# Modulation columns moved in the weight plan, and four stages of a two-block kernel reordered

## The reference

```python
# first block
mix = jax.nn.sigmoid(gate_na) * y_na + jax.nn.sigmoid(gate_hg) * y_hg   # y_na = attention @ w_na_out
h = h + mix @ w_o[l]                                                    # y_hg = recurrence @ w_hg_out
m = rms_norm(h, norm_mlp[l])
h = h + jnp.square(jax.nn.relu(m @ w_up[l])) @ w_down[l]
# modulation, once in each layer of the second block; c is one vector of 1024
ada = jax.nn.silu(c) @ ada_w + ada_b
shift, scale, gate = jnp.split(ada, 3, axis=-1)
h = rmsnorm(x, norm_g) * (1.0 + scale[:, None, :]) + shift[:, None, :]
# even layer: a window sum over 2, 4, 8 or 16 tokens less the token itself, by groups of 256 columns
outs.append(win_sum / count[None, :, None] - af[..., sl])
z = jnp.einsum('hts,bnshd->bnthd', w, vh) + b_s.T[None, None, :, :, None]   # w is masked, lower triangle
# odd layer
yc = rmsnorm(yc, gla_norm_g).reshape(B_, S, GLA_VW)      # yc: gated linear attention
y = jnp.concatenate([yc, yd], axis=-1) * jax.nn.silu(gate)
```

## Time and profile before

| what | us |
|---|---|
| median of 3 runs | 856.7 |
| the three runs | 856.07, 856.7, 861.47 |
| the profiled execution | 856.8 |
| its span, from the first instruction to the last | 854.8 |
| TensorE busy in the span | 830.4 |
| VectorE busy | 629.7 |
| ScalarE busy | 490.9 |
| GpSimd busy | 109.5 |

### The profile page before, as it was taken

One profiled execution on the slowest core, in us unless ns is written; L12 is line 12 of the kernel. 1 busy time (PEld: TensorE's weight loads), 2 busy tenths in 40 slices (PEclk: granted clock), 3 DMA queues, 4 the chain that ended last, 5 costly groups with the idle time before them and its releaser, 6 DMA issues.

```text
span 854.8 us, 16987 instructions
## 1 busy us (share of the span) xinstructions
PE 830.4 (97%) x6904; PEld 807.8 (95%) x6904; DVE 629.7 (74%) x1002; ACT 490.9 (57%) x876; POOL 109.5 (13%) x130
## 2 busy tenths in 40 slices
PE   5999999999999999999999999999999999999996
PEld 5998899997998999999999999999999999999996
DVE  5676578982899788787999687786888558455663
ACT  6454456664556656564666663544677356666652
POOL 0010255320112000000030420000202030000001
PEclk9999999999999999999999999999999999999999
DMA  9833334453468898989777456565655436544431
GB/s 352 319 100 117 120 124 128 146 179 97 145 225 289 289 389 270 382 281 384 268 250 280 148 184 207 172 198 177 195 160 185 124 102 212 164 156 155 148 103 50
DMA packets 46876, 170.40 MB, mean 199 GB/s; under 512 B 5200, under 2 KB 5456, under 8 KB 46544
## 3 DMA queue, kind: packets, MB, share of 16 engines
q1 hardware_dynamic: 46080, 165.31, 58.3%
q10 hardware_dynamic: 720, 4.01, 1.2%
HBM read 168.26 MB, written 1.05 MB: 198 GB/s over the span
## 4 chain that ended last, share of the span: by engine, by line
PE 82%; DVE 10%; ACT 4%; issue 2%; DMA 1%; POOL 0%; SPq 0%; DVEq 0%; POOLq 0%; ACTq 0%
PE bank L194 81%; DVE wl L233 5%; DVE raw L221 1%; ACT wh L203 1%; DMA raw<-in_ws 1%; DVE B1l L221 1%; ACT L209 1%; PE bank L197 0%; ACT sq L200 0%; DVE A L221 0%; DVE B0l L233 0%; ACT B1h L200 0%; DVE B1l L233 0%; ACT th L200 0%; DVE h L221 0%
## 5 line engine op out<-in xcount | busy, mean ns | idle before, releaser
L233 DVE TENSOR_TENSOR wl<-raw,wh 128x1024 fp32r<-128x1024 f32 x259 | 327.5, 1276 | 21.8 <-ACT wh L203 21.0
L203 ACT CAST wh<-raw 128x1024 fp32r<-128x1024 f32 x259 | 268.9, 1048 | 120.7 <-PE bank L194 60.4
L194 PE MATMUL bank<-XAh,wl 128*128 128x256 f32 (+1 forms) x896 | 255.8, 285 | 2.7 <-DVE wl L233 2.1
L194 PE MATMUL bank<-XAl,wh 128*128 128x256 f32 (+1 forms) x896 | 249.9, 279 | 0.0
L194 PE MATMUL bank<-XAh,wh 128*128 128x256 f32 (+1 forms) x896 | 249.8, 279 | 0.0
L194 PEld LDWEIGHTS bank<-XAh,wl 128*128 128x128 f32 x896 | 168.7, 188 | 6.0 <-DVE wl L233 2.7
L194 PEld LDWEIGHTS bank<-XAl,wh 128*128 128x128 f32 x896 | 169.3, 189 | 0.0
L194 PEld LDWEIGHTS bank<-XAh,wh 128*128 128x128 f32 x896 | 168.7, 188 | 0.1
L194 PE MATMUL bank<-B1h,wl 128*128 128x256 f32 (+1 forms) x464 | 130.7, 282 | 3.3 <-DVE wl L233 2.1
L194 PE MATMUL bank<-B1h,wh 128*128 128x256 f32 (+1 forms) x464 | 129.8, 280 | 0.0
L194 PE MATMUL bank<-B1l,wh 128*128 128x256 f32 (+1 forms) x464 | 129.7, 280 | 0.0
(11 more groups left out here) (261 smaller groups left out, 1228.0 us busy)
## 6 DMA issues: line engine op xcount, KB each, us to landing
raw<-in_ws SPq DMA_DIRECT2D x307, 512.0 KB, 4.4
bias<-in_bias ACTq DMA_DIRECT2D x1, 1664.0 KB, 12.0
hK<-in_xk SPq DMA_DIRECT2D x4, 272.0 KB, 4.8
h<-in_xt ACTq DMA_DIRECT2D x1, 1088.0 KB, 6.4
out<-gc SPq DMA_DIRECT2D x4, 256.0 KB, 2.6
C<-in_cst SPq DMA_DIRECT2D x1, 512.0 KB, 7.6
crow<-in_crow ACTq DMA_DIRECT2D x1, 512.0 KB, 3.5
wT<-in_wt SPq DMA_DIRECT2D x1, 512.0 KB, 6.5
```

Of the source, the lines that this page charges most:

```text
L194: return self.real.matmul(*a, **k)
L203: return self.real.copy(*a, **k)
L233: return self.real.tensor_tensor(*a, **k)
```

## The change

Five edits, none of which alters what is computed or how many products there are.

1. The line in `plan` that places the 48 items "a". Before, they stand after units 58 to 121 (six of nine units) and then after every third unit to 135. After, five stand after units 46 to 50, none from 51 to 70, the same six of nine from 71 to 121, then five after the even units 140 to 148, and three after 159, 162 and 165.
2. `w_na_out` (four units) goes ahead of the last four units of the gates, columns 5632 to 6144, on all engines. ScalarE gets a `table(EXP_SET)` behind the recurrence's root, since tanh now follows it; with it the later `table(LN_SET)` ahead of the MLP becomes a real load, where before the table with ln was still there.
3. The pooled groups take one more step each, and on VectorE the low parts come one step behind `pf`. The four steps that `sgu` waited for at its start go. The mask of `wT` goes ahead of `vn`.
4. The eight last tiles of linear attention take two steps each and not one; the low part follows its own tile.
5. The unread tile `qp` goes. One of the same size is put at the start of `pna` (`bp`) and one ahead of `vn` (`vp`), so that tiles between them move by 128 bytes.

```diff
@@ plan
-    mat("w_in", 3584, 6144)
+    mat("w_in", 3584, 5632)
     mat("w_na_out", 0, 1024, nk=4)
+    mat("w_in", 5632, 6144)
     mat("w_hg_out", 0, 1024, nk=4)
...
-        if ada and (58 <= n < 122 and n % 9 in (0, 2, 3, 4, 6, 8) or 122 <= n < 144 and n % 3 == 0):
+        if ada and (46 <= n < 51 or 71 <= n < 122 and n % 9 in (0, 2, 3, 4, 6, 8) or 140 <= n < 149 and n % 2 == 0
+                    or 158 <= n and n % 3 == 0):
@@ tiles
-        qp = sbt(ph1, "qp", [128, 32])
...
+        bp = sbt(pna, "bp", [128, 32])
...
+        vp = sbt(ph3, "vp", [128, 32])
@@ vector_program (tensor, scalar and gpsimd alike)
-            tiles("g20", "w_in", 5632, 6144, g20, t0=16)
...
             tiles("na", "w_na_out", 0, 1024, na_mix, nk=4)
+            tiles("g20", "w_in", 5632, 6144, g20, t0=16)
             w.drain()
@@ scalar_program, recurrence
                     e.activation(v, v, ACT.Exp, scale=-0.5).then_inc(*up("ro_rs", r))
+                table(EXP_SET)
                 yield
@@ pool_side, tensor, scalar and gpsimd
-                    for _ in range(2 + g // 2):
+                    for _ in range(3 + g // 2):
                         yield
@@ pool_side, vector
                     e.tensor_tensor(p[:, :, 0:16], p[:, :, 0:16], src[:, :, 16:32], ALU.subtract).then_inc(
                         *up("pf", g))
+                    yield
                     for n in range(2):
                         low((B1h[:, 2 * g + n, 0:256], B1l[:, 2 * g + n, 0:256]), p[:, n, :], ("p_high", 2 * g + n),
...
-            rows("vn", "even_in", 2048, 3072)
             e.wait_ge(one["wT"], 16)
             e.tensor_tensor(wT[:, :, :], wT[:, :, :], bc(cst_("tril"), [[0, 8], [1, 128]]), ALU.mult).then_inc(
                 *up("wT", 0))
+            rows("vn", "even_in", 2048, 3072)
@@ sgu, tensor, scalar and vector (gpsimd: scaled(12) becomes scaled(8))
-                for _ in range(4):
-                    yield
                 for hh in range(8):
@@ gla, vector (tensor, scalar and gpsimd: one more yield for each j)
                     e.scalar_tensor_tensor(o, o, hp[:, 12 + j:13 + j], gc[:, j, :], ALU.mult, ALU.mult).then_inc(
                         *up("go_gated", j))
-                    if j:
-                        gla_low(j - 1)
-                    yield
-                gla_low(7)
+                    yield
+                    gla_low(j)
+                    yield
```

More of the change, by code:

```diff
@@ L951, in tensor_program @@
             w.steps = 2
-            t_tiles("g20", "w_in", 5632, 6144, X, X_of("mix"), g20_free, t0=16)
             t_tiles("na", "w_na_out", 0, 1024, (B0h, B0l),
                     lambda k: [("na_high", k), ("na_low", k)], lambda t: [("na_mix", t)], nk=4)
+            t_tiles("g20", "w_in", 5632, 6144, X, X_of("mix"), g20_free, t0=16)
             w.drain()
@@ L1460, in scalar_program @@
             w.steps = 2
+            tiles("na", "w_na_out", 0, 1024, nothing, nk=4)
             tiles("g20", "w_in", 5632, 6144, g20, t0=16)
-            tiles("na", "w_na_out", 0, 1024, nothing, nk=4)
             w.drain()
@@ L2647, in gpsimd_program @@
             w.steps = 2
+            tiles("na", "w_na_out", 0, 1024, nk=4)
             tiles("g20", "w_in", 5632, 6144, t0=16)
-            tiles("na", "w_na_out", 0, 1024, nk=4)
             w.drain()
@@ L2687, in gpsimd_program @@
             w.rows("vn", "even_in", 2048, 3072, nothing, nothing, lambda col: squares("fin")((6, 7) if col else range(6)))
-            w.side.append(scaled(12))
+            w.side.append(scaled(8))
             tiles("ga", "even_in", 3072, 4096)
```

## The result

The changed kernel takes 846.1 us (median of four executions: 853.3, 846.14, 846.06, 842.98) against 856.67 before in the same session: a ratio of 0.988, 95% interval 0.985 to 0.991. Forecast was 847.5. The profiled execution, though, is the one of 853.3 us, and it explains the spread.

A forecast was written before the change was run, and what follows sets the result against it. TensorE's products bound the kernel, so only its waits could go: 4.00 + 1.35 + 2.16 + 0.85 + 1.72 = 10.1 us off 856.8, 0.8 given back, gives 847.5 us. Range 842.5 to 853.5.

The forecast's parts named there:

- Waits, not products: Whole kernel: products stay, so only TensorE's waits can go; seven inside, from 225.91 to 714.87, all ended by VectorE.
- the half clock: At 268.36 to 271.78, after the longest inside wait, granted clock 0.50; its going was to gain 1.71 us.
- 0.8 given back for thin margins: Taken off the summed gain for the wait at 239.70 and one of 708.23 and 714.87, by half.
- the slow rhythm: Rival: the stretches at 113 ns per product slow down, 2173 products pay 9.8 us, 857.3 us; chance 0.04.
- The columns: Moving modulation items out of 240 to 268 and 419 to 442 gains 4.00 and 1.35 us.
- the new columns make the gating stage late: Rival in 474 to 500: VectorE at 23.4 of 26.00 us, ScalarE's chain between; 853.4 us, chance 0.06.
- The last rival: The number of columns is the same, so waits only move to where they go: 856 us; chance 0.03.
- The output projection: Ahead of the last gates, it removes the waits before 225.91 and 239.70: 2.16 us gained.
- thin margin: Wait of 0.62 us at 239.70, VectorE full from 222.2 to 240: 0.79 us counted as gone.
- Table loads: Two more on ScalarE, 1.28 us each with no drain; nothing taken, 0.64 us if the first came through.
- Pooled parts, linear attention: New order in 474 to 500 gains 0.85 us, in 693 to 719 1.72 us.
- The rhythm: TensorE's 113.4 or 117.9 ns per product with nothing waiting; which one can't be derived, no change taken.

The follow-up runs named there:

- e1: Kernel before with only the new places of the 48 items "a" in `plan`: 856.4 us, ratio 0.9985.
- e2: Kernel before with only `w_na_out` ahead of the last four gate units and the added `table(EXP_SET)`: 853.8 us, ratio 0.996.
- e3: Kernel before with only the new order of the pooled groups, the mask and the last linear-attention tiles: 855.0 us, ratio 0.999.
- e6: Changed kernel with the 48 items "a" back at their old places in `plan`: 852.3 us.
- e9: Changed kernel with pooled groups, mask and the gating unit's start as before: 851.3 us, executions from 847.9 to 856.7.
- e11: Kernel of e5 with the last linear-attention tiles two to a unit again, as before the change: 847.46 us.
- e4: Changed kernel with the unread tiles as before (`qp` back, `bp` and `vp` out): 847.0 us, two of six near 853.
- e5: Changed kernel with VectorE doing the last pair of the mix ahead of the low part of unit 58: 845.75 us, median of twelve executions.

## Why the prediction was right, point by point

*Waits, not products.* Right. All seven waits and the half clock went. From before to the changed kernel the medians differ by 10.5 us; the sum had 10.1 less 0.8. The 0.8 given back for thin margins wasn't needed: without it the sum is 846.7, and the middle group lies at 846.1. The terms don't stand by themselves, though: put into the kernel before one at a time, edit 1, edit 2 and edits 3 with 4 gain 0.3, 2.8 and 1.7 us, 4.8 in sum, and together 10.5. With one edit alone, part of what it won was lost again, in a new wait (486 and 498.79 in e1, 294 in e2, 297 in e3's profile) or to the slow rhythm; together the edits left none of these waits.

*The columns.* The term was 5.35 us; taking edit 1 out of the changed kernel (e6) costs 6.1. That five columns beside the recurrence cost nothing is shown by e1, whose wait for `B0l` there is what it was. But alone the edit is worth nothing (e1), since the columns' other new home, the gates of the even layer, can't take them without edit 3. Here my text had the right rival with the wrong weight: "the new columns make the gating stage late", up to 5.0 us lost. e1 and e9 lost it, 5.1 us in e9, by the mechanism named, VectorE waiting for ScalarE with `wl` behind. In the changed kernel edit 3 prevents it. The last rival, that the waits only move to where the columns go (856), is what edit 1 alone did.

*The output projection.* The term was 2.16; edit 2 alone measured 2.8, with 0.8 us of the next wait and 1.7 of half clock going along, 1.0 given back to the rhythm and 0.8 to the new wait at 294. The "thin margin" at 239.70 was right: 0.20 of the 0.62 us stayed. Its price was not: I gave back half of that place, 0.4 us, but behind the 0.2 us that stayed three of ten executions ran 7 us longer.

*Table loads.* I held to the row's 1.28 us with nothing behind it, against the 2.66 us of the Trainium skill's "ScalarE: Activation LUTs", section "What ACT_TABLE_LOAD costs". The two new loads measured 1.28, and the next instruction followed within 0.02 us. No run here shows the page's drain.

*Pooled parts, linear attention.* For edit 4 the term was 1.72 and e11 measured 1.7. Edits 3 and 4 alone (e3) measured 1.7 too, in medians that mix two groups, so that edit 3's own 0.85 isn't seen. The wait of 0.68 went, but the 91 products behind it that had run at 113.4 ns stayed at 118: half of the term was given back. Edit 3's worth is what it does for edit 1.

*The rhythm.* Half luck, and the step that fell short: "Which one a stretch takes, I can't derive; I take no change", with 0.04 for the slow rhythm and 0.12 for the fast as if one of them would be the kernel's. Both came, in different executions of one program: 3 of 10 near 853.4, 2 of 10 near 842.9, the rest from 845.5 to 846.2, up to 2 us under the forecast. The median was right since most executions keep the fast rhythm in the MLP. The sign that I had named for it, no waits and yet over 850 us with fewer products between 272 and 437, is what both profiles show, but for the 0.20 us in the weight loads. And a sign stood in the table ahead of the prediction: of the three runs before, 861.47 is one of the upper group. My argument "272 to 437 kept it for 1453 products" was half of it: one execution that keeps a rhythm says nothing of the next, and a break of 0.2 us was enough to lose it.

*Still open.* Why one restart leaves 113.4 and the next 118 ns isn't settled: equal breaks gave both, at unit 57 (0.31 us between products: 118 in the changed kernel, e2 and e9, 113.4 in e4 and e6) and before 225.9 (a wait of 1.2 us: 113.4 in the kernel before, 118 in e3, whose code is the same up to there). Why it turns without a break, as in e9, isn't settled either. Addresses aren't needed for it. Nor did I see a profile of an execution near 842.5, so which stretch is fast there is a guess: the one from 482 to 603, at 118 ns in all profiles of the changed kernel and of e5 and fast from 494 on in e9's, has the products for 3.4 us.

## What to carry to other kernels

When a kernel is bound by TensorE, look at products per microsecond stretch by stretch beside the waits: here a wait of 0.2 us, which stands among the waits of the weight loads alone, went with 7 us in some executions. Work that is moved out of a full stage needs a place where order, not only the sum of busy time, has room; edits of such a pair should be priced together and taken out one at a time. And take several executions before trusting the one that was profiled.

## What the runs showed of the hardware

- TensorE did the same 128 x 128 x 256 product at 113.4 or at 118 ns with no wait in sight and the granted clock at 1.00. A rhythm held for up to some 1450 products. It changed at breaks of 0.2 us and more (unit 57, 237.09), at small products between (269.87 in e1), and also with no break at all (494.3 in e9; at the start of the gates of the even layer in all fourteen traces).
- The waits of 2.12 us (before), 2.13 (e6) and 3.36 (e1) were each followed within 0.9 us by a granted clock of 0.50, 1.2 GHz, for 3.4 us; in the wait of 3.38 (e9) it fell 1.3 us before the wait's end and stayed for 6.8. The waits of 1.31 (e2) and 1.32 (e3) at the place of the first had none behind them.
- The changed kernel's eleven table loads took 1283 ns each, and eight of them were followed by ScalarE's next instruction within 0.02 us; behind the other three ScalarE waited for a DMA, VectorE and TensorE.
